# Layer 0 of a three-layer block: output products and a weight split written inside the last pairs of heads

## The reference

```python
    oa = _map_query_blocks(lambda q1, q2: _diff_attend(q1, q2, k1, k2, va, lam), lq1, lq2)
    ob = _map_query_blocks(lambda q: _softmax_attend(q, kb, vb), lqb)
    new_lat = x_lat + g_a * _merge_heads(oa, ob, lam_init, diff_subln, w_out)
    h = _modulate(_rmsnorm(new_lat), sh_f, sc_f)
    new_lat = new_lat + g_f * _swiglu(h, w_ffn_in, w_ffn_out)
```

## Time and profile before

| | |
|---|---|
| runs, us | 2381.36, 2379.24, 2378.86; median 2379.24 |
| profiled execution | 2380.3 us, span 2378.5 us, mean granted TensorE clock 0.991 |
| busy share of the span | PE 96%, weight loads 78%, DVE 66%, ACT 39%, POOL 15% |
| DMA | 257.70 MB, mean 108 GB/s |
| matmuls of the output products (L1274, L1275, L1277), with the chain's share | 1% of the span each |
| PE's idle time in all, from span and busy time | 97.4 us |

### The profile page before, as it was taken

How to read it: one execution, slowest core, us unless ns; L and a number is a source line. 1 busy time by engine, 2 the same in 40 slices (tenths; PEclk the granted TensorE clock), 3 DMA queues, 4 the chain that set the end, 5 groups by cost and what they waited for, 6 DMA issues and landing times.

```text
span 2378.5 us, 34983 instructions
## 1 busy us (share of the span) xinstructions
PE 2281.1 (96%) x14058; PEld 1865.5 (78%) x14058; DVE 1562.5 (66%) x2497; ACT 933.8 (39%) x1768; POOL 350.6 (15%) x455
## 2 busy tenths in 40 slices
PE   6999899999999899899999999999999999999998
PEld 3876567888888788777888888888887778888886
DVE  3548686666667662487779875656474877765457
ACT  4336454422212521477342232332352774423333
POOL 0110100001022210001000413223112120101131
PEclk9999999999999999999999999999999999999999
DMA  7430024654444322110422333224122112432321
GB/s 269 136 110 10 19 81 176 245 181 161 161 151 152 106 71 82 64 70 22 157 68 97 134 124 124 94 102 139 48 80 80 38 52 109 160 107 89 106 89 71
DMA packets 79473, 257.70 MB, mean 108 GB/s; under 512 B 5712, under 2 KB 10832, under 8 KB 70864
## 3 DMA queue, kind: packets, MB, share of 16 engines
q1 hardware_dynamic: 65888, 207.84, 25.4%
q0 software_dynamic: 12704, 46.14, 5.5%
q10 hardware_dynamic: 720, 1.47, 0.2%
HBM read 246.00 MB, written 9.44 MB: 107 GB/s over the span
## 4 chain that ended last, share of the span: by engine, by line
PE 48%; DVE 4%; ACT 2%; issue 1%; POOL 0%; POOLq 0%; DVEq 0%; ACTq 0%
PE PS L1305 8%; PE PS L1306 8%; PE PS L1307 8%; PE PS L1376 4%; PE PS L1377 4%; PE PS L1378 4%; PE PS L1182 1%; PE PS L1223 1%; PE PS L1274 1%; PE PS L1277 1%; PE PS L1275 1%; PE PS L1201 1%; PE PS L1016 1%; PE PS L1014 1%; PE PS L1013 1%
## 5 line engine op out<-in xcount | busy, mean ns | idle before, releaser
L1305 PE MATMUL PS<-HH,WH 128*128 128x512 f32 (+1 forms) x1088 | 420.3, 386 | 3.2 <-DVE WL L2383 1.8
L1306 PE MATMUL PS<-HL,WH 128*128 128x512 f32 (+1 forms) x1088 | 416.7, 383 | 0.0
L1307 PE MATMUL PS<-HH,WL 128*128 128x512 f32 (+1 forms) x1088 | 416.7, 383 | 0.0
L2794 ACT ACTIVATE WH<-STG 128x1024 fp32r<-128x1024 f32 (+1 forms) x202 | 196.9, 1022 | 269.7 <-PE PS L1378 224.9
L2383 DVE TENSOR_TENSOR WL<-STG,WH 128x1024 fp32r<-128x1024 f32 (+1 forms) x202 | 241.2, 1235 | 37.2 <-ACT WH L2794 37.1
L1305 PEld LDWEIGHTS PS<-HH,WH 128*128 128x128 f32 x1088 | 204.4, 188 | 47.9 <-issue 6.3
L1905 DVE SCALAR_TENSOR_TENSOR ACC<-ADAW,CS,ACC 128x1024 f32<-128x1024 f32 x168 | 227.1, 1387 | 21.6 <-PE PS L1016 14.4
L1307 PEld LDWEIGHTS PS<-HH,WL 128*128 128x128 f32 x1088 | 204.4, 188 | 40.5
L1306 PEld LDWEIGHTS PS<-HL,WH 128*128 128x128 f32 x1088 | 204.5, 188 | 39.7 <-issue 1.0
L1376 PE MATMUL PS<-WH,AH 128*128 128x512 f32 x600 | 234.9, 392 | 0.3 <-DVE AL L2611 0.3
L1377 PE MATMUL PS<-WL,AH 128*128 128x512 f32 x600 | 233.6, 389 | 0.0
(11 more groups left out here) (276 smaller groups left out, 4411.9 us busy)
## 6 DMA issues: line engine op xcount, KB each, us to landing
STG<-in_w_up SPq DMA_DIRECT2D x66, 1024.0 KB, 6.0
ADAW<-in_w_ada SPq DMA_DIRECT2D x96, 512.0 KB, 3.9
STG<-in_w_down SPq DMA_DIRECT2D x20, 1024.0 KB, 5.2
ADAW<-in_w_ada POOLq DMA_DIRECT2D x32, 512.0 KB, 4.1
STG<-in_w_ffn_out SPq DMA_DIRECT2D x10, 1024.0 KB, 6.9
STG<-in_ev_w_in SPq DMA_DIRECT2D x8, 1024.0 KB, 5.2
STG<-in_w_in SPq DMA_DIRECT2D x6, 1024.0 KB, 6.3
spill<-X POOLq DMA_DIRECT2D x10, 512.0 KB, 5.1
```

The source lines that it names most:

```text
L1305: e.matmul(out, h_, hh, start=c == 0, stop=False)
L1306: e.matmul(out, h_, hl, start=False, stop=False)
L1307: return e.matmul(out, l_, hh, start=False, stop=c == 7)
L2794: return e.activation(dst, src, ACT.Copy)
```

## The change

The output products (0,0) and (1,0) move from `w_out` into the tail of `pairs`: TensorE makes (0,0) after turn 29 and (1,0) after turn 31, ahead of the product with values of pair 15. They take PSUM banks 0 and 1, which are freed by the exponentials of head 30. ACT makes the high part of tile 0 ahead of its copy of turn 29, the high part of tile 1 and the four high parts of the second weight half ahead of its copy of turn 30; DVE makes the low part of tile 0 ahead of the normalisation of head 31, that of tile 1 and two low parts of weights ahead of its copy of turn 30, the other two ahead of its copy of turn 31. The high parts of tiles 0 to 2 change places in memory, since keys and values are still in use where that of tile 0 stood. Layers 1 and 2 keep their order. What is computed is the same.

```diff
@@ def out_parts(self, L, i):
-        o = (10240, 11264, 0)[out_place(i)]
+        o = ((0, 10240, 11264) if L == 0 else (10240, 11264, 0))[out_place(i)]
@@ TensorE, pairs
         late_turn(n - 3)
+        for b in range(4):
+            freed[b] = [k.ac_exp((a.name, n - 2 + b // 2))]
+        rot["set"], rot["n"] = list(range(8)), 0
+        out_product(0, 0, 0)
+        late_turn(n - 2)
         a.out_pair(len(items) - 2, 5, items[-2]["v"])
-        late_turn(n - 2)
         late_turn(n - 1)
+        out_product(0, 1, 0)
         a.out_pair(len(items) - 1, 5, items[-1]["v"])
         a.close()
@@ TensorE, w_out (the product itself is now the function out_product)
-        for i, n in out_order(L):
+        for i, n in out_order(L)[2 if L == 0 else 0:]:
@@ DVE, pairs
+        out_low(0, 0)
         normal(name, L, n - 1, items[-1]["nk"], 5)
-        for i in (n - 3, n - 2, n - 1):
-            pt_tail(name, L, i, items[i // 2]["nkt"], 5, 3)
+        pt_tail(name, L, n - 3, 6, 5, 3)
+        out_low(0, 1)
+        out_weights_low(0, 1, 0, 0)
+        out_weights_low(0, 1, 0, 1)
+        pt_tail(name, L, n - 2, 6, 5, 3)
+        out_weights_low(0, 1, 1, 0)
+        out_weights_low(0, 1, 1, 1)
+        pt_tail(name, L, n - 1, 6, 5, 3)
@@ DVE, w_out (ACT likewise, with out_high and out_weights_high)
-        for i in range(3):
-            low(i)
-        for h in range(2):
+        for i in range(2 if L == 0 else 0, 3):
+            out_low(L, i)
+        for h in range(2 if L else 0):
             for i in range(2):
                 out_weights_low(L, 1, h, i)
@@ ACT, out_weights_high
-            w.wait_ge(*k.pe_proj(("qup", 1, 5)))
+            w.wait_ge(*(k.pe_score(("B", 31)) if n else k.pe_proj(("qup", 1, 5))))
@@ ACT, out_high
+        if L == 0 and i < 2:
+            w.wait_ge(*k.pe_score(("B", 31)))
+            w.wait_ge(*k.ac_cat(tt))
+            w.wait_ge(*k.ac_out(("B", 12 + i)))
@@ ACT, pairs
+        out_high(0, 0)
         pt_head(n - 2)
+        out_high(0, 1)
+        for h in range(2):
+            for i in range(2):
+                out_weights_high(0, 1, h, i)
+        pt_head(n - 1)
         result(p - 1)
-        pt_head(n - 1)
         pt_head(n)
         result(p)
```

More of the change, by code:

```diff
@@ L1103, in close @@
         def close(self):
-            for b in range(4):
-                freed[b] = [k.ac_exp((self.name, self.n - 1))]
             freed[4] = [k.ac_ptc((self.name, self.item[("turned", 0)]))]
@@ L1255, in pairs, with out_product @@
         late_turn(n - 3)
+        for b in range(4):
[3 more added lines that the diff above has]
+        late_turn(n - 2)
         a.out_pair(len(items) - 2, 5, items[-2]["v"])
-        late_turn(n - 2)
         late_turn(n - 1)
+        out_product(0, 1, 0)
         a.out_pair(len(items) - 1, 5, items[-1]["v"])
         a.close()
+    def out_product(L, i, n):
+        tt = WOUT_TT[L][i]
+        xh, xl = k.out_parts(L, i)
+        b = take(("wo", L, tt, n))
+        for c in range(8):
+            wh, wl = k.out_weights(L, n, c // 4)
+            x = slice(c * P, (c + 1) * P)
+            w.wait_ge(*k.ac_xh((L, tt, c // 4)))
+            w.wait_ge(*k.dv_wolo((L, n, c // 4, c % 4 // 2)))
+            e.matmul(PS[:, b, :], xh[:, x], wh[:, c % 4, :], start=c == 0, stop=False)
+            e.matmul(PS[:, b, :], xh[:, x], wl[:, c % 4, :], start=False, stop=False)
+            w.wait_ge(*k.dv_xl((L, tt, c // 4)))
+            m = e.matmul(PS[:, b, :], xl[:, x], wh[:, c % 4, :], start=False, stop=c == 7)
+        m.then_inc(*k.pe_wout.up((L, tt) if n else (L, tt, 0)))
+        freed[b] = [k.dv_yg(("wo", L, tt, n))]
     def w_out(L, bg):
@@ L1264, in w_out @@
             w.wait_ge(*x(("att", L)))
-        for i, n in out_order(L):
+        for i, n in out_order(L)[2 if L == 0 else 0:]:
             tt = WOUT_TT[L][i]
[L1267 to L1279, removed]
+            out_product(L, i, n)
             if n:
@@ L1553, in tensor_program @@
     pairs(a, items, bg)
-    rot["set"], rot["n"] = list(range(8)), 0
     e.drain().then_inc(*k.pe_end.up(("att", 0)))
@@ L2219, in out_weights_low, with out_low @@
                         ALU.subtract).then_inc(*k.dv_wolo.up((L, n, h, i)))
+    def out_low(L, i):
+        xh, xl = k.out_parts(L, i)
+        tt = WOUT_TT[L][i]
+        for h in range(2):
+            x = slice(h * 512, h * 512 + 512)
+            w.wait_ge(*k.ac_xh((L, tt, h)))
+            e.tensor_tensor(xl[:, x], k.x(tt)[:, x], xh[:, x].bitcast(F32), ALU.subtract).then_inc(*k.dv_xl.up((L, tt, h)))
     def pairs(name, L, bg):
@@ L2392, in after @@
                 layer_norm("a", L, tt, [k.dv_x(("wo", L, tt, 1))])
-        def low(i):
-            xh, xl = k.out_parts(L, i)
-            tt = WOUT_TT[L][i]
-            for h in range(2):
-                x = slice(h * 512, h * 512 + 512)
-                w.wait_ge(*k.ac_xh((L, tt, h)))
-                e.tensor_tensor(xl[:, x], k.x(tt)[:, x], xh[:, x].bitcast(F32), ALU.subtract).then_inc(*k.dv_xl.up((L, tt, h)))
         def regain(i):
@@ L2455, in w_out @@
             for x in out_made(L)[i]:
-                low(x)
+                out_low(L, x)
             if L and i != last - 1:
@@ L2978, in out_weights_high, with out_high @@
         if L == 0:
-            w.wait_ge(*k.pe_proj(("qup", 1, 5)))
+            w.wait_ge(*(k.pe_score(("B", 31)) if n else k.pe_proj(("qup", 1, 5))))
         w.wait_ge(*k.ring_in[h](("wo", L, n)))
         copy(hi[:, x, :], k.ring(L, h, 4, 512)[:, x, :]).then_inc(*k.ac_wohi.up((L, n, h, i)))
+    def out_high(L, i):
+        xh, _ = k.out_parts(L, i)
+        tt = WOUT_TT[L][i]
+        if L == 0 and i < 2:
+            w.wait_ge(*k.pe_score(("B", 31)))
+            w.wait_ge(*k.ac_cat(tt))
+            w.wait_ge(*k.ac_out(("B", 12 + i)))
+        if i >= 3:
+            w.wait_ge(*k.pe_wout((L, WOUT_TT[L][out_place_before(i)])))
+        for h in range(2):
+            x = slice(h * 512, h * 512 + 512)
+            copy(xh[:, x], k.x(tt)[:, x]).then_inc(*k.ac_xh.up((L, tt, h)))
     def pairs():
@@ L3125, in norm @@
                 layer_norm("a", L, tt)
[L3127 to L3134, removed]
         for s in k.ends(("att", L)):
             w.wait_ge(*s)
-        for i in range(3):
-            high(i)
-        for h in range(2):
+        for i in range(2 if L == 0 else 0, 3):
+            out_high(L, i)
+        for h in range(2 if L else 0):
             for i in range(2):
@@ L3144, in w_out @@
             for x in out_made(L)[i]:
-                high(x)
+                out_high(L, x)
             if i == last:
```

## The result

| | before | changed |
|---|---|---|
| median of 7 runs each, us | 2379.86 (2378.86 to 2381.36) | 2386.32 (2385.33 to 2388.44) |
| ratio, 95% interval | | 1.0023 (1.0014 to 1.0032) |
| profiled execution / span, us | 2380.3 / 2378.5 | 2386.31 / 2384.5 |
| mean granted clock | 0.991 | 0.988 |

A forecast was written before the change was run, and what follows sets the result against it. TensorE, busy 96% of the span, was taken as the bound. A late conditioning chain (1.3 us) plus low clock (1.7) made 3.0 us slower: 2382.2 against the median of 2379.24, range 2376.8 to 2386.0.

The forecast's parts named there:

- What the products gain: TensorE from turn 29 to L860: moved products fill waits, 3.3 us gained; attention ends at 380.9, L860 ready at 392.5.
- The chain behind attention: DVE's conditioning blocks 4 to 7 start after attention's later end and hold L860: 397.3 instead of 395.92, 1.3 us lost.
- The landing: Time from POOL's issue of conditioning block 6 until it lands, behind four loads of old x: taken as 5.7 us.
- a rival: Block 6 lands with block 7, 7.1 us after issue; clock low for 6.9: 6.1 us slower, 2385.3; chance 0.20.
- The clock: After TensorE's one-piece wait of 4.7 us at L860 the clock falls to half: 1.7 us lost, bounds 0 and 3.4.
- The sum: Whole kernel: 1.3 us for the late chain plus 1.7 for the clock, 3.0 us slower.
- "Same": Whole kernel's time within about 0.2% (4.8 us) of no change: chance 0.77.

The follow-up runs named there:

- experiment 6: Changed kernel, DVE adding conditioning blocks 4 and 5 inside attention, POOL issuing blocks 6 and 7 behind its drain: 2379.28 us, kernel before beside it 2380.65.
- 12: The kernel of experiment 6 run again, beside the changed kernel on the same chip: 2378.52 us, kernel before beside it 2380.57.
- experiments 2: Changed kernel with only TensorE's L860 moved behind product (2,0): 2380.46 us, kernel before beside it 2380.52.
- experiment 4: Changed kernel with product (1,0) put back after attention, only (0,0) inside: 2377.32 us, kernel before beside it 2380.52.
- Experiment 3: Changed kernel with POOL issuing conditioning blocks 6 and 7 ahead of its four loads of old x: 2385.72 us, kernel before beside it 2380.52.
- Experiment 7: experiment 4 with DVE's copy of turn 31 ahead of the last two low parts of weights: 2380.86 us, kernel before beside it 2380.65.
- the filler: Changed kernel with 24 useless matmuls on TensorE between product (1,1) and L860: 2384.35 us, kernel before beside it 2380.65; its trace was not read.
- run 9: The changed kernel measured and profiled again, unaltered: 2386.38 us, kernel before beside it 2380.57.
- experiment 8: Kernel before with DVE adding conditioning blocks 4 and 5 after its copy of turn 31, POOL issuing 6 and 7 behind its drain: 2382.44 us against 2380.65.
- experiment 1: Changed kernel, DVE adding conditioning blocks 4 and 5 inside attention and POOL issuing blocks 6 and 7 there: 2382.9 us, kernel before beside it 2380.52.
- 10: The kernel of the filler run again, for a readable trace: 2385.05 us, kernel before beside it 2380.57.

## Why the prediction was right or wrong

- **What the products gain.** Right. Attention's last product ended at 376.91 + 1.53 = 378.44; with the 2.52 us that this profile is early, 380.96, forecast 380.9. TensorE was ready for L860 at 396.26 - 6.20 = 390.06, or 392.58, forecast 392.5. The gain of 3.3 us was there, and experiments 6 and 12 collect it in the stretch (3.4 and 2.9).
- **The chain behind attention.** Right in its mechanism: DVE's blocks behind the end of attention release L860, shown by experiments 2, 4 and 6, which each take the wait away by another end. Block 6 was issued at 382.56, or 385.08, forecast 385.1.
- **The landing.** Here is the term that was mis-sized. The prediction took 5.7 us and kept 7.1 for a rival; it was 7.3. Hence a wait of 6.20 instead of 4.7, and L860 2.86 later instead of 1.3. The row of 5.7 was of a load behind SP's traffic; the new place is behind four loads on POOL's own queue. The row of the fourth of those loads, 6.1, was the nearer one, with block 6 the fifth in the same row; but it too would have been short, since that fourth load now took 7.6 us. Experiment 3 shows the order at work: as the first of the row, block 6 landed after 4.2 us. The Trainium skill (DMA: Bandwidth & Descriptors, "Issuing engines are not separate DMA queues") says that transfers of all engines interleave on the same 16 DMA engines. Experiment 7 agrees: with SP's 1 MB in flight, POOL's first load took 5.5 us instead of 3.8. The rule says nothing of how long a load behind others takes, and so gave no support to 5.7 against 6.1.
- **The clock.** Right in its mechanism: the filler shows it is the standing that lets it fall. The size, 1.78 us lost in the stretch (4.64 - 2.86) against 1.7 forecast, is in part luck: waits of much the same length cost 2.30 us in run 9 and 2.18 in experiment 3. The Trainium skill (TensorE: Matmul & The Clock Gate, "What's actually happening") says that the clock is set by how busy TensorE has been of late, and is halved when it was idle. The traces agree: 0.50 behind the wait of 6.12 us, 1.00 with the filler in it.
- **The sum.** 3.0 forecast in the stretch, 4.64 there. The median moved by 6.5 and, the second time, by 5.8 us, with stretches 4.64 and 5.32 us longer than before. So 0.5 to 1.8 us lie outside the stretch. The same holds for the other kernels of the table: against before, each median but that of experiment 4 moved by 0.7 to 2.0 us more than its stretch did, also in experiment 8, where no product is moved. Behind the stretch lie 1968.56 us in the first profile of before and 1971.98 in the second, 1972.44 and 1970.75 in the two of the changed kernel; ahead of it the load's issue came at 365.21, 363.91, 362.69 and 366.90. Single profiles thus differ by more than what is sought, and whether the changed kernel loses there steadily stays open.
- **Chances.** "Same" had 0.77 and slower by over 0.2% 0.20, by a block that lands after 7.1 us with the clock low for 6.9. That block came, but the clock cost 1.78 us and not the 3.4 of that rival; it was the part outside the stretch, in no term of the prediction, that brought the medians over the bound, and the interval leaves open whether they are over it.

## What to carry to other kernels

Work that is moved ahead of a step's end moves the end itself: before counting the gap that it fills, read what else starts only at that end, and how far ahead of its reader each such chain was. Here one was 0.56 us ahead. The end of attention came 8.7 us later, the splits moved away gave that chain only part of this back, and TensorE was at its reader 3.3 us sooner: so the chain became the bound. Moving that chain as well, or moving less, turned a loss of 6 us into a gain of 1.4 to 3.2.

## What the runs showed of the hardware

- POOL's drain ended about 1 us after the landing of the load issued just ahead of it, in two cases: in experiment 1 it took 6.41 us with a landing after 5.3, in the kernel before 5.16 us with a landing after 4.1. That it waits for the landing is the plain reading, not a test. Put ahead of the issues, it cost TensorE nothing (experiment 6). The row from before:

```profile
L3560 POOLq DRAIN  x1: 5164/5164/5164, 359.3 to 359.3; - x1
```

- In the changed kernel and in experiments 2, 4 and 10, the first of POOL's loads of 512 KB landed 3.8 to 4.1 us after its issue and the fifth, issued 3.1 us after the first, 5.8 to 7.3. In experiment 7, with SP's load of 1 MB issued 0.6 us ahead, it was 5.5 and 7.6. Meanwhile the core moved 401 to 418 GB/s in the changed kernel (382 to 388).
- 5.5 us of useless matmuls in TensorE's wait kept the granted clock at 1.00 and made the stretch 1.7 us shorter (49.37 to 47.64).
